# SBUF layout in which every large buffer begins on a multiple of 512 bytes, in a two-block transformer kernel on one core

## What is computed

```
# first block
mod  = silu(c) @ w_ada + b_ada                 # 6 vectors of 2048
proj = modulate(rms(x)) @ w_in                 # u, q, k, v
y    = concat(s5_mixer(u), dilated_attention(q, k, v))
x    = x + gate1 * (y @ w_out)
x    = x + gate2 * ((silu(h2 @ w_ffn_gate) * (h2 @ w_ffn_up)) @ w_ffn_down)
# second block, two layers (attention over tokens and a context of 256, then a Fourier mixer)
x    = post_norm(x, attention_mixer(modulate(x), modulate(ctx)), gate)
x    = post_norm(x, fourier_mixer(modulate(x)), gate)
# fourier_mixer: (fft2(u).real * silu(gate)) @ w_out
```

## Time and profile before

| | |
|---|---|
| median of three timed runs | 2555.1 us |
| the profiled execution, first to last instruction | 2558.8 us |
| TensorE busy in it | 2433.2 us, 95% |
| VectorE, ScalarE busy | 65%, 41% |
| mean granted TensorE clock | 0.979 of full speed |
| HBM | 229 GB/s over the span |

### The profile page before, as it was taken

One profiled execution on the slowest core, in us unless ns is written; L12 is line 12 of the kernel. 1 busy time (PEld: TensorE's weight loads), 2 busy tenths in 40 slices (PEclk: granted clock), 3 DMA queues, 4 the chain that ended last, 5 costly groups with the idle time before them and its releaser, 6 DMA issues.

```text
span 2558.8 us, 37889 instructions
## 1 busy us (share of the span) xinstructions
PE 2433.2 (95%) x15430; PEld 2064.7 (81%) x15430; DVE 1654.1 (65%) x1869; ACT 1043.7 (41%) x1386; POOL 220.0 (9%) x198
## 2 busy tenths in 40 slices
PE   5899989989999999999999999999979999999995
PEld 1588765569888888998887887888768999999894
DVE  8655545457888888885776566455764575755547
ACT  2444764234333333333433454444433334333431
POOL 0139700020000000000111000000011000000000
PEclk9899999999999999999999999999989999999998
DMA  9855479958999999996553753333545585765551
GB/s 388 315 158 158 138 272 389 402 194 323 355 349 347 360 353 372 364 343 212 159 172 116 238 153 116 100 98 120 192 137 186 186 288 175 251 195 171 165 165 41
DMA packets 257582, 589.44 MB, mean 230 GB/s; under 512 B 20608, under 2 KB 29824, under 8 KB 256128
## 3 DMA queue, kind: packets, MB, share of 16 engines
q1 hardware_dynamic: 257408, 587.02, 66.3%
HBM read 584.85 MB, written 2.10 MB: 229 GB/s over the span
## 4 chain that ended last, share of the span: by engine, by line
PE 88%; DVE 4%; DMA 3%; ACT 2%; issue 1%; POOL 1%; SPq 0%; DVEq 0%; ACTq 0%
PE psum L208 13%; PE psum L220 12%; PE psum L209 12%; PE psum L210 12%; PE psum L221 12%; PE psum L222 12%; PE psum L292 3%; DMA start_slots<-in_w_ada 2%; PE psum L2496 1%; PE psum L1881 1%; DVE wlo L197 1%; PE psum L482 1%; PE psum L2472 1%; PE psum L2471 1%; PE psum L1895 1%
## 5 line engine op out<-in xcount | busy, mean ns | idle before, releaser
L197 DVE TENSOR_TENSOR wlo<-raw,whi 128x1024 fp32r<-128x1024 f32 (+2 forms) x728 | 881.1, 1225 | 571.8 <-ACT whi L191 567.0
L191 ACT CAST whi<-raw 128x1024 fp32r<-128x1024 f32 (+2 forms) x728 | 737.0, 1022 | 952.6 <-PE psum L222 497.9
L220 PE MATMUL psum<-hh,whi 128*128 128x256 f32 x2688 | 761.1, 283 | 4.9 <-DVE wlo L197 4.4
L221 PE MATMUL psum<-hh,wlo 128*128 128x256 f32 x2688 | 752.1, 280 | 0.0
L222 PE MATMUL psum<-hl,whi 128*128 128x256 f32 x2688 | 752.1, 280 | 0.0
L220 PEld LDWEIGHTS psum<-hh,whi 128*128 128x128 f32 x2688 | 509.1, 189 | 22.1 <-issue 11.2
L222 PEld LDWEIGHTS psum<-hl,whi 128*128 128x128 f32 x2688 | 511.1, 190 | 0.0
L221 PEld LDWEIGHTS psum<-hh,wlo 128*128 128x128 f32 x2688 | 507.1, 189 | 1.9 <-issue 1.0
L208 PE MATMUL psum<-whi,hh 128*128 128x512 f32 (+1 forms) x720 | 292.2, 406 | 9.9 <-DVE wlo L197 6.6
L210 PE MATMUL psum<-whi,hl 128*128 128x512 f32 (+1 forms) x720 | 281.8, 391 | 0.0
L209 PE MATMUL psum<-wlo,hh 128*128 128x512 f32 (+1 forms) x720 | 281.4, 391 | 0.0
(11 more groups left out here) (382 smaller groups left out, 2297.7 us busy)
## 6 DMA issues: line engine op xcount, KB each, us to landing
araw<-in_ada_w SPq DMA_DIRECT2D x128, 512.0 KB, 6.5
raw<-in_w_in_fourier SPq DMA_DIRECT2D x128, 512.0 KB, 3.8
raw<-in_w_ffn_gate SPq DMA_DIRECT2D x88, 512.0 KB, 9.1
raw<-in_w_ffn_up SPq DMA_DIRECT2D x88, 512.0 KB, 7.9
raw<-in_w_ffn_down SPq DMA_DIRECT2D x88, 512.0 KB, 9.8
raw<-in_w_in_attn SPq DMA_DIRECT2D x88, 512.0 KB, 4.4
araw<-in_w_ada SPq DMA_DIRECT2D x80, 512.0 KB, 7.3
start_slots<-in_w_ada SPq DMA_DIRECT2D x64, 512.0 KB, 8.3
```

What stands on the lines that cost most here:

```text
L191: nc.scalar.copy(whi[:, u % SPLITS, 0:kn, 0:w], raw[:, u % RING, 0:kn, 0:w]).then_inc(s_hi, 1)
L197: nc.vector.tensor_tensor(wlo[:, u % SPLITS, 0:kn, 0:w], raw[:, u % RING, 0:kn, 0:w], whi[:, u % SPLITS, 0:kn, 0:w].bitcast(F32), ALU.subt ...
L220: nc.tensor.matmul(o, h, hh[:, kt + k], start=(kt + k == 0 and f % 2 == 0), stop=False)
L221: nc.tensor.matmul(o, lw, hh[:, kt + k], start=False, stop=False)
```

## The change

No instruction is added, removed or moved: the instruction lists of the five engines are the same, row by row. Only start addresses differ. A filler of 384 bytes goes ahead of `raw`; `cond_windows` and the 64-byte `pad` leave their place between `araw` and `powers`; `h32` moves behind the small tiles, and ahead of it come `cond_windows` and a filler of 480 bytes.

```diff
+    fill = sb(ctx, "fill", [P, 96])
     raw = sb(ctx, "raw", [P, RING, 2, CW])
...
     araw = sb(ctx, "araw", [P, 4, 2, CW])
-    condz = sb(ctx, "cond_windows", [P, 2, KT, 35])
-    pad = sb(ctx, "pad", [P, 16])
     powers = sb(ctx, "powers", [P, 2, CW])
...
-    h32 = sb(ctx, "h32", [P, 2, 2, S])
     aim2 = sb(ctx, "aim2", [P, 2, 2, PAIRS])
...
     onez = sb(ctx, "ones_window", [P, 64])
+    condz = sb(ctx, "cond_windows", [P, 2, KT, 35])
+    fill2 = sb(ctx, "fill_2", [P, 120])
+    h32 = sb(ctx, "h32", [P, 2, 2, S])
```

## The result

The change made the kernel slower: median 2572.88 us of four runs against 2555.24 us of four runs of before taken with them, ratio 1.0057 with a 95% interval of 1.0044 to 1.0070. The forecast was 2539 us, a gain. 2572.9 lies inside the stated range of 2496 to 2577, but the sign was wrong.

A forecast was written before the change was run, and what follows sets the result against it. TensorE was taken as the bound, busy 2433 of 2559 us, so each large matmul's step carries to the end. Terms -11.0 (a) and -5 (c), the others 0, summed to -16 us: 2555.1 to 2539, range 2496 to 2577.

The forecast's parts named there:

- (a): Lines 208 to 210, stationary `hidh`, `ctxh`, `ckvTh` and low parts leaving 32 mod 64: 2208 matmuls gain 5 ns, -11.0 us.
- (b): Lines 208 to 210, stationary `hh` and `hl` from 64 to 0 mod 512: taken 0, bounds -26 and +11 us.
- (c): Lines 220 to 222, `hh` streaming over `whi`, 8064 matmuls at two paces: taken -5 us, bounds -18 and +18.
- (d): Loads, now landing at multiples of 512: taken 0, with 1.5 us either way.
- (e): ScalarE and VectorE casts and remainders: addresses cost nothing, taken 0, durations unchanged within 4 ns.
- Slower: streaming and stationary operand now collide: Lines 208 to 222: both operands at the same rest mod 512 slow the matmuls; 2575 us, chance 0.26.
- Much faster: Large matmuls: both operands on a multiple of 512, steps fall towards 216 ns; 2500 us, chance 0.19.
- No change: The 5 ns come with something other than rest mod 64, or feed-forward savings become waits; 2555 us, chance 0.18.

The follow-up runs named there:

- the first experiment: Layout of before plus a 288-byte filler ahead of `h32`, so `h32` and everything over it begin at 0 mod 512; 2556.42 us, ratio to before 0.9997.
- the fifth run: Changed layout with `powers`, `hh`, `hl`, `x` and the small tiles at 192 mod 512, all else at 0; 2540.31 us, ratio to before 0.9931.

## Why the prediction was wrong

The reading of the bound was right. TensorE's steps carry the end, and in the runs worked out above the time follows from steps times counts to within about 2 us.

**(a)** hit in sign and nearly in size: 11.0 us said, 14.3 measured (12.0 + 2.3). The reason given was wrong, so the sign was no merit of the reasoning. The three buffers at 224 differ from `hh` in their rest mod 64 and also in their distance from `whi`, and I took the first. The first experiment took `hidh` from 32 to 0 mod 64 with `whi` left at 128. That gave 1.5 ns (2.7 us), the difference between the distances 96 and 128 in the table above, and its time cannot be told from before.

**(b)** was taken at 0 and measured -2.5 us, within its bounds; the ground for the 0, that multiples of 64 are alike, was wrong: `hh` at distance 64 or 128 has 233 ns.

**(c) is the step that failed**: "Taken: -5 us", bounded by -18 and +18. Measured +30.6 us, where (a) and (b) together gained 16.8. The two paces were read as the two ends of what these lines can do, so the worst case was all of them at 118 ns. A third pace, 120 ns, is what equal starts (distance 0) give, and then no stretch is fast. That the pace "is not tied to an address by any row" was true of the rows; it was no ground for a value on the side of a gain. The stretch that the earlier trace rows show changes its pace at one layout, but which paces exist is a matter of the distance: of the eight distances only 64 bytes under `whi` has 113 ns as a common pace (at 64 bytes above it a few stretches have it, at the others none), and the kernel before stood on it. Any move of `hh` against `whi` to another of the eight would have lost it, by the table at a price of 0.6 to 3.9 ns on each of 8064 matmuls.

**(d)** was taken at 0 with 1.5 us either way, on the ground that 394 and 387 GB/s showed no price of the start. The rate of the first 100 us rose by 2% (394 to 403), and that of the second stretch of the earlier trace rows, between the same two times, from 387 to 394. TensorE's waits for `start_slots` fell from 34.2 to

```profile
PE psum L293 <- DMA start_slots<-in_w_ada: 32.4, 19, 10.7
```

but they are 33.0 in the first experiment, at 394 GB/s, and 33.7 in the fifth, at 402, so this fall is not shown to be the loads'.

The Trainium skill's page "DMA: Bandwidth & Descriptors", section "How a descriptor splits into AXI transactions", has one transaction more for a descriptor that does not start on 256 bytes. It tells this of what a transaction reads, and here the start of the destination was moved; 64 and 128 slow, 0 and 256 fast has the same 256 bytes in it, but no run shows that this rule is the reason.

**(e)** held: the cast into `hidh` 616 ns as in the earlier trace rows, its remainder 684:

```profile
L1652 ACT CAST hidh<-hid x38: 612/616/618, 609.4 to 2522.0; 128x512 fp32r<-128x512 f32 x38
L1658 DVE TENSOR_TENSOR hidl<-hid,hidh x38: 681/684/1793, 613.3 to 2522.7; 128x512 fp32r<-128x512 f32 x38
```

**The rivals.** "Slower: streaming and stationary operand now collide" had the sign, a chance of 0.26 and 2575 us, 2 us off. That nearness is luck: its terms were 0 for (a), +11 for (b) and +9 for (c), and the steps gave -14.3, -2.5 and +30.6. Its mechanism is half right: equal distance is the second worst of eight in lines 220 to 222, and the best of eight in lines 208 to 210. What I set against it, that plain fp32 shows 379 ns for like and unlike starts, holds for plain fp32, from start to start as well (215 to 216 ns in lines 1881, 976 and 2496), and says nothing of fp32r, where the operand streams at twice the rate; that reservation stood in the text and should have weighed more. "Much faster" fell, as nothing came near 216 ns. "No change" named the cause, "the distance between the operands", but only to say that the 5 ns would stay. The change moves every one of these distances (`hidh` less `whi` from 96 to 0, `hh` less `whi` from 192 to 0, modulo 256), so by that very cause there was no ground for 2555. The Trainium skill's page "SBUF — State Buffer", section "Specifications (TRN2)", has lines of 16 bytes, by which no start here would matter; the runs show 6 ns between distances that are all multiples of 32, so as an account of TensorE's reads it isn't enough.

## What to carry to other kernels

Aligning everything alike is not neutral: where matmuls in fp32r run back to back, the distance between the streaming and the stationary buffer modulo 256 bytes was worth up to 2.9% of such work in one direction of the product and 3.8% in the other (227.5 to 234.1 ns, 115.6 to 120.0 in the mean), and the two directions want different distances (0 and 192). Give a buffer that is used in both roles the distance that suits its more frequent one, and try all eight multiples of 32, with each step measured from start to start. Destinations of large loads on 256 bytes gained 2% in rate here. Where rows show a correlation with an absolute start, write down every relation that changes with it before pricing one of them.

## What the runs showed of the hardware that was not expected

- The step of an fp32r matmul goes with the distance of its operands modulo 256. Moving all by 64 or 256 bytes leaves every step within 0.1 ns (a move of all by 32 was not tried), moving `hh` and `hl` alone changes 8064 steps by 4.2 ns in the mean.
- Lines 220 to 222 have two paces, 113 and 118 ns, within one execution in layouts with `hh` 64 bytes under `whi`, and 120 ns nearly throughout at distance 0. In the five kernels with `hh` 64 bytes under `whi`, 202 of 205 runs of over 72 such matmuls with no other matmul between them keep one pace from their first to their last, so in nearly all of them the pace is settled as the run begins, and 37% (before) to 51% (the fifth run) of the matmuls in long runs are at the fast one. What decides it was not tried.
- Loads into destinations at 0 mod 256 moved 401 to 404 GB/s in the first 100 us (twelve kernels), at 64 or 128 mod 256 394 GB/s (three).
